# A decoder layer with 32 experts on one core: the gather leaves out empty slots, the adding up of a block moves behind the next block's first weight chunk, and ScalarE's exponential and logarithm share one table set

## The chip, the core and the metric

The kernel runs on one core of a Trainium2 chip. The core has a matrix engine (TensorE, PE in the profile, its weight loads PEld), a vector engine (VectorE, DVE), an engine for functions and copies (ScalarE, ACT), a general engine (GpSimd, POOL), an engine that issues transfers (SyncE, SP), and 16 DMA engines between HBM and the on-chip memory SBUF. PE writes its results to another on-chip memory, PSUM, of 8 banks of 512 fp32 columns for 128 partitions. Engines run their own instruction lists and meet at semaphores. The metric is the device time of one execution in microseconds (us).

## What is computed

One layer of a decoder for 288 tokens (256 of a prompt, 32 of eight samples) of width 2048, in fp32. A condition vector scales and shifts the tokens, one projection feeds two kinds of attention of 8 heads each, and w_o maps them back; a layer norm follows. Then each token goes to two of 32 experts:

```python
def hier_moe(u, w_gr, b_gr, w_er, b_er, w_gate, w_up, w_down):
    ...
    g_idx = jnp.argmax(g_logits, axis=-1)
    ...
    top_val, top_idx = lax.top_k(e_sel, TOP_K)
    gate = g_w * jax.nn.softmax(top_val, axis=-1)
    eid = g_idx[:, None] * EXPERTS_PER_GROUP + top_idx
    dense_gate = jnp.sum(jax.nn.one_hot(eid, N_EXPERTS, dtype=jnp.float32) * gate[..., None], axis=1)
    y = jnp.zeros((B * T, D), jnp.float32)
    for e in range(N_EXPERTS):
        hid = jax.nn.silu(h @ w_gate[e]) * (h @ w_up[e])
        y = y + dense_gate[:, e:e + 1] * (hid @ w_down[e])
    return y.reshape(B, T, D).astype(u.dtype)
```

The second group of heads ("stick breaking") needs log(1 + exp(-|z|)) and exp of a difference for each head.

## The kernel before

**Ahead of the experts.** All weights come through a ring of eight 1 MB slots (`ring`), loaded by SP in a fixed order. After the projections, eight heads of stick breaking run one after the other (h = 0 to 7): PE makes the logits, DVE scales them (L1541), ACT computes |z|, exp and ln(1 + ...) (L1148 to L1150), DVE adds (L1546, L1547), PE sums over keys, DVE subtracts (L1552), ACT takes the exponential (L1156), PE multiplies with the values. The sample tokens' part is woven in (L1159 to L1170 on ACT, L848 on PE). A normalisation over heads follows (ACT L1183 to L1190, DVE L1593 to L1597), then w_o and a layer norm. An activation function works only while its table set is active; the build puts an ACT_TABLE_LOAD ahead of each activation whose set is not.

**The plan.** DVE and PE route the tokens. The (token, expert) pairs are sorted by expert into blocks of B = 64 slots, an expert's pairs filling the block's slots from slot 0 up. `plan` holds each block's expert and the number of blocks (25 here), `idxs` the token of each slot (64 rows, one column for each block and one for the empty block behind the last). A slot that no pair fills has token 0.

**The loop over blocks** (L1010 on PE, L1248 on ACT, L1753 on DVE, L526 on POOL, L352 on SP). For block i:
- SP loads the expert's 12 chunks of 1 MB (`put_expert`): four of w_gate, four of w_up into `ring`, four of w_down into `mslot`. Chunk c is issued when PE has used chunk c of the block before (`moe_used`), so 12 chunks are the whole buffer.
- POOL gathers the block's 64 token rows of 8 KB from HBM into `xg` (64 partitions) by an indirect DMA (L520), as soon as PE has turned the rows of the block before out of `xg`; PE turns them one block later.
- PE multiplies the eight gate and up chunks (L1017), turns the next block's rows (`turn_rows`, L971), adds up the block before (`combine`, L999 and L1005: a matrix that holds each slot's token and weight maps 64 rows to 288 tokens), turns the hidden rows (L1028) and multiplies the four down chunks (L1036).
- DVE multiplies silu(gate) by up (`hid`, L1758), adds the five pieces of `combine` to the outputs in SBUF (`add_up`, L1744 to L1751), copies the turned hidden rows (`hT`, L1762), builds the next matrix (L1765 to L1771) and copies half of the down result (`yout`, L1773). ACT takes silu (L1252), copies the next block's turned rows (L1245) and the other half of `yout` (L1255).

The last block is added up behind the loop. A second layer norm ends the kernel: ACT copies the sample sums (L1262), POOL, DVE and ACT work on three tiles of tokens, with a logarithm and an exponential of one column for each tile (L1268, L1269).

Blocks run as hardware loops of 40 rounds, of which those from 25 on do nothing; order within an engine is the order of the code.

## Time and profile before

| what | before |
|---|---|
| median of three timed runs | 1931.15 us (1924.26 to 1936.56) |
| the profiled execution, its own time | 1920.6 us |
| its span, first to last instruction | 1918.9 us |
| mean granted TensorE clock, share of full speed | 0.938 |
| busy share of the span: PE, PEld, DVE, ACT, POOL | 86%, 50%, 28%, 13%, 6% |
| moved by the DMA engines | 545.31 MB, mean 284 GB/s |
| ACT_TABLE_LOAD in the loop | 25, 1283 ns each |

Busy shares are averages over stages with different limits. A row of a timeline gives the start and the length of a run of instructions, and in brackets how long the engine had been idle and what ended that. The chain of waits is followed back from the last instruction; its share by line says what set the end.

### The profile page before, as it was taken

The page shows a single profiled execution, that of the slowest core. Times are in us where ns is not written, and L with a number is a line of the kernel's source. Part 1 is how long each engine was busy: PE and PEld are TensorE (multiplying, and loading weights), DVE is VectorE, ACT ScalarE, POOL GpSimd, SP SyncE. Part 2 cuts the span into 40 slices and gives each one's busy share as a digit, 9 for nine tenths or more (in the row PEclk, how much of TensorE's full clock was granted, in tenths as well). Part 3 has the DMA queues.
Part 4 walks back from the last instruction along what each step waited for, and adds up shares of the span by engine and source line. Part 5 has one row for each costly group of instructions (what it writes and reads, how often), then busy time and mean ns, then how long its engine had stood idle before and what let it go on. Part 6 is the DMA issues. An engine that isn't in the chain of part 4 may idle for free.

```text
span 1918.9 us, 24776 instructions
## 1 busy us (share of the span) xinstructions
PE 1641.1 (86%) x9583; PEld 965.5 (50%) x9583; DVE 532.9 (28%) x881; ACT 250.4 (13%) x330; POOL 119.7 (6%) x155
## 2 busy tenths in 40 slices
PE   3689999999999996679968998888888888888870
PEld 0046666436787654557744564444444444444430
DVE  0010038602212213420055213131312222131328
ACT  0000012000000013630024110101010010101004
POOL 3000000001111000000020000000000000000004
PEclk8679999999989997889987999999999999999985
DMA  9988888773424353423323999999999999999961
GB/s 357 421 361 327 322 311 322 314 287 133 151 87 142 136 183 127 176 98 127 116 104 116 361 408 390 405 390 407 392 404 402 395 406 391 406 389 406 389 259 49
DMA packets 78909, 545.31 MB, mean 284 GB/s; under 512 B 9170, under 2 KB 9346, under 8 KB 16338
## 3 DMA queue, kind: packets, MB, share of 16 engines
q1 hardware_dynamic: 72146, 507.62, 67.2%
q0 software_dynamic: 6384, 34.73, 6.1%
q10 hardware_dynamic: 336, 2.36, 0.3%
q8 instruction: 31, 0.51, 0.1%
q14 instruction: 12, 0.10, 0.0%
HBM read 532.87 MB, written 11.80 MB: 284 GB/s over the span
## 4 chain that ended last, share of the span: by engine, by line
DMA 33%; PE 17%; DVE 4%; ACT 2%; issue 1%; SPq 1%; DVEq 0%; ACTq 0%
DMA ring<-w_up 33%; PE ps L893 7%; PE ps L1017 5%; PE ps L1036 1%; SPq L355 1%; PE ps L999 1%; PE ps L907 1%; ACT arena L1227 0%; DVE shift L1785 0%; DVE arena L1625 0%; PE ps L885 0%; PE ps L884 0%; DVE arena L1593 0%; PE ps L917 0%; PE ps L981 0%
## 5 line engine op out<-in xcount | busy, mean ns | idle before, releaser
L1017 PE MATMUL ps<-ring,arena 128*64 128x256 f32 x3200 | 376.4, 385 | 51.0 <-DMA ring<-w_up 45.2
L1017 PEld LDWEIGHTS ps<-ring,arena 128*64 128x64 f32 x3200 | 241.7, 138 | 190.8 <-DMA ring<-w_up 83.7
L577 PE MATMUL ps<-arena,ring 128*128 128x288 f32 x1280 | 322.0, 410 | 0.0
L577 PEld LDWEIGHTS ps<-arena,ring 128*128 128x128 f32 x1280 | 240.8, 191 | 89.8 <-issue 25.5
L1036 PE MATMUL ps<-arena 128*64 128x512 f32 x800 | 177.2, 594 | 23.6 <-DVE arena L1762 23.6
L561 PE MATMUL ps<-ring,silu_c 128*32 128x512 f32 x768 | 116.8, 719 | 53.5 <-DMA ring<-w_ada 27.4
L893 PE MATMUL ps<-arena,ring 128*128 128x288 f32 x512 | 128.3, 410 | 10.6 <-DVE arena L1593 10.6
L999 PE MATMUL ps<-arena 64*128 64x512 f32 x400 | 109.6, 633 | 24.3 <-DVE arena L1751 15.1
L1036 PEld LDWEIGHTS ps<-arena 128*64 128x64 f32 x800 | 66.2, 137 | 118.5 <-issue 90.6
L1758 DVE TENSOR_TENSOR arena<-arena,ps 128x256 f32<-128x256 f32 x25 | 10.5, 421 | 404.9 <-PE ps L1017 404.9
L893 PEld LDWEIGHTS ps<-arena,ring 128*128 128x128 f32 x512 | 98.3, 192 | 38.5 <-DVE arena L1593 11.1
L585 PE MATMUL ps<-ring,arena 128*128 128x512 f32 x256 | 113.4, 596 | 1.3 <-ACT arena L1075 1.3
L561 PEld LDWEIGHTS ps<-ring,silu_c 128*32 128x32 f32 x768 | 20.4, 118 | 130.4 <-DMA ring<-w_ada 71.0
L585 PEld LDWEIGHTS ps<-ring,arena 128*128 128x128 f32 x256 | 47.4, 190 | 62.6 <-issue 59.4
L999 PEld LDWEIGHTS ps<-arena 64*128 64x128 f32 x400 | 39.0, 190 | 75.0 <-issue 75.0
L1748 DVE TENSOR_TENSOR arena<-arena,ps 128x1024 f32<-128x1024 f32 x50 | 60.7, 1213 | 0.4 <-PE ps L999 0.4
L1773 DVE COPY arena<-ps 128x512 f32<-128x512 f32 x25 | 17.3, 691 | 148.9 <-PE ps L1036 148.9
L520 POOL DMA_INDIRECT arena<-u_rows,idx x26 | 24.3, 936 | 543.8 <-PE ps L971 542.9
L1255 ACT COPY arena<-ps 128x512 f32<-128x512 f32 x25 | 14.6, 585 | 330.1 <-PE ps L1036 330.1
L1252 ACT ACT_TABLE_LOAD x25 | 32.1, 1283 | 179.7 <-PE ps L1017 179.7
L1245 ACT COPY arena<-ps 128x1024 f32<-128x1024 f32 x26 | 26.3, 1012 | 222.1 <-PE ps L971 222.1
L1750 DVE TENSOR_TENSOR arena<-arena,ps 128x512 f32<-128x512 f32 x50 | 34.3, 687 | 54.3 <-PE ps L999 54.2
(403 smaller groups left out, 1288.8 us busy)
## 6 DMA issues: line engine op xcount, KB each, us to landing
ring<-w_gate SPq DMA_DIRECT2D x100, 1024.0 KB, 29.2
ring<-w_up SPq DMA_DIRECT2D x100, 1024.0 KB, 29.9
arena<-w_down SPq DMA_DIRECT2D x100, 1024.0 KB, 23.4
ring<-w_ada SPq DMA_DIRECT2D x96, 1024.0 KB, 8.2
ring<-w_in SPq DMA_DIRECT2D x56, 1024.0 KB, 6.3
ring<-w_o SPq DMA_DIRECT2D x16, 1024.0 KB, 5.1
ring<-cache_k SPq DMA_DIRECT2D x16, 512.0 KB, 4.2
ring<-cache_v SPq DMA_DIRECT2D x16, 512.0 KB, 4.2
```

The costliest lines, as they stand in the source:

```text
L520: nc.gpsimd.indirect_dma_start(out=xg, out_offset=None, in_=u2_rows[:], in_offset=bass.IndirectOffsetOnAxis(idx1[:, 0:1], 0)).then_inc(gat ...
L561: last = mm(ps[32 * j:32 * j + 32, 0, :], silu_c[:, t, :], ring[:, slot, 512 * j:512 * (j + 1)], start=(t == 0), stop=(t == KC - 1))
L577: last = mm(ps[:, bank, 0:T], ring[:, slot, P * t:P * (t + 1)], uT[:, t, :], start=(t == 0), stop=(t == KC - 1))
L585: mm(ps[:, 4 + i, :], uT[:, 4 * (c % 4) + t, t0:t0 + tn], ring[:, slot, 512 * t:512 * (t + 1)], start=(c % 4 == 0 and t == 0), stop=(c % 4 ...
L893: last = mm(ps[:, 4 + m % 4, 0:T], ring[:, n % SLOTS, P * k:P * (k + 1)], mixT[:, k, :], start=(k == 0), stop=(k == KC - 1))
L999: last = mm(ps[0:tn, ((7, 4), (5, 6))[j % 2][r], :], spread[rows, t0:t0 + tn], yout[rows, 512 * (j % 2):512 * (j % 2 + 1)], start=True, st ...
L1017: last = mm(ps[B * s:B * (s + 1), 2 + c // 4, 0:256], xgT[:, 4 * (c % 4) + t, :], ring[:, c, 512 * t + 256 * s:512 * t + 256 * (s + 1)], s ...
L1036: last = mm(ps[B * s:B * (s + 1), 5 + nn, :], hT[:, q % 2, B * (q // 2):B * (q // 2 + 1)], mslot[q][:, 1024 * s + 512 * nn:1024 * s + 512 ...
L1245: nc.scalar.copy(xgT, ps[:, 0:2, :].rearrange("p a (m s) -> p (a m) s", s=B)).then_inc(x_copied, 1)
L1252: A(hsil, ps[:, 2, 0:256], ACT.Silu).then_inc(sil_act, 1)
L1748: v.tensor_tensor(w, w, ps[:, 5:7, :], ALU.add).then_inc(sum_dve, 1)
L1750: v.tensor_tensor(w[:, 0], w[:, 0], ps[:, 7, :], ALU.add)
```

## The change

Three things change.

*The gather.* An index of an empty slot becomes EMPTY = 1024 instead of 0, which lies beyond the 288 rows; the indirect DMA has a bounds check of T - 1 = 287 that leaves such rows out. To make the index, DVE sums token - 1024 over the pairs of a slot and adds 1024 back (L1713 before, a tensor_scalar now); the first slot is held to at most 287 (`rowlim`), so one row is always moved. POOL fills `xg` with zeros once ahead of the first gather; a slot that is left out keeps what an earlier block left there, and its weight in the adding up is zero.

*The loop.* `combine(i)` on PE moves from behind `turn_rows` to behind chunk 0 of the gate weights; `add_up(i)` on DVE moves from behind `hid` to ahead of it.

*The tables.* ACT loads the set `natural_log_exp_and_others` once at the start, the set of Silu once ahead of the loop, and the first one again behind the loop.

```diff
@@ gather (POOL) @@
+            g.memset(rowlim[:], EMPTY)
...
+            link(g.memset(rowlim[0:1, :], T - 1.0))
...
                 nc.gpsimd.indirect_dma_start(out=xg, out_offset=None, in_=u2_rows[:],
-                                             in_offset=bass.IndirectOffsetOnAxis(idx1[:, 0:1], 0)
-                                             ).then_inc(gathered, 16)
+                                             in_offset=bass.IndirectOffsetOnAxis(idx1[:, 0:1], 0),
+                                             bounds_check=T - 1, oob_is_err=False).then_inc(gathered, 16)
...
             pool.wait_ge(tt_act, 24)
+            link(g.memset(xg, 0.0))
             gather(1)
@@ plan (DVE) @@
-                    link(v.tensor_tensor(tokid[:], tokid[:], vm, ALU.mult))
+                    link(v.tensor_scalar(tokadd[:], tokid[:], -EMPTY, None, ALU.add))
+                    link(v.tensor_tensor(tokadd[:], tokadd[:], vm, ALU.mult))
...
-            v.tensor_copy(idxs[:], ps[0:B, 4, 0:NB1]).then_inc(plan_ready, 1)
+            v.tensor_scalar(idxs[:], ps[0:B, 4, 0:NB1], EMPTY, rowlim[:, 0:1], ALU.add, ALU.min
+                            ).then_inc(plan_ready, 1)
@@ loop (PE) @@
                         last.then_inc(moe_used, 1)
+                        if c == 0:
+                            with pe.If(i > 0):
+                                combine(i)
                     turn_rows(i + 2)
-                    with pe.If(i > 0):
-                        combine(i)
@@ loop (DVE) @@
+                    with dve.If(i > 0):
+                        add_up(i)
                     dve.wait_ge(sil_act, i + 1)
...
                     v.tensor_tensor(hid, hsil, ps[:, 3, 0:256], ALU.mult).then_inc(hid_dve, 1)
-                    with dve.If(i > 0):
-                        add_up(i)
@@ tables (ACT): at the start, ahead of the loop, behind the loop @@
+            nc.scalar.preload_act_table_set("natural_log_exp_and_others")
...
+            nc.scalar.preload_act_table(ACT.Silu)
...
+            nc.scalar.preload_act_table_set("natural_log_exp_and_others")
```

How it stands in the engines' lists, where the names in brackets are the semaphores waited for. PE in the loop before, from the last up chunk (L1017, chunk 7) over the turning of rows (L971) to the first matmuls of `combine` (L999):

```order
L1017 MATMUL ps<-ring,arena 64x256 [waits moe_loaded7]
L1017 MATMUL ps<-ring,arena 64x256 x7
L968 ISA
L971 MATMUL ps<-ident,arena 128x64 [waits gathered]
L971 MATMUL ps<-ident,arena 128x64 x15
L1022 COMPARE_AND_BRANCH
L990 ISA
L993 ISA [waits spread_ready,y_evac]
L999 MATMUL ps<-arena 128x512 [waits sum_dve]
```

PE in the changed kernel, from the first gate chunk (L1023, chunk 0) to the same matmuls (now L1005):

```order
L1023 MATMUL ps<-ring,arena 64x256 [waits moe_loaded0]
L1023 MATMUL ps<-ring,arena 64x256 x7
L1028 COMPARE_AND_BRANCH
L996 ISA
L999 ISA [waits spread_ready,y_evac]
L1005 MATMUL ps<-arena 128x512 [waits sum_dve]
```

The five pieces of `combine`, with their wait for the copies of the block before (`y_evac`), now stand between chunk 0 and chunk 1; behind chunk 7 the turning of rows is followed at once by the wait for `hid_dve`.

ACT at the first two heads before: |z| (L1148), exp (L1149), ln (L1150), and the exponential of the difference (L1156):

```order
L1148 ACTIVATE arena<-arena 128x384 [waits z_dve,small_loaded]
L1149 ACTIVATE arena<-arena 128x384 [waits act_step]
L1150 ACT_TABLE_LOAD
L1150 ACTIVATE arena<-arena 128x384 [waits act_step]
L1148 ACTIVATE arena<-arena 128x384 [waits z_dve]
L1149 ACT_TABLE_LOAD
L1149 ACTIVATE arena<-arena 128x384 [waits act_step]
L1150 ACT_TABLE_LOAD
L1150 ACTIVATE arena<-arena 128x384 [waits act_step]
L1156 ACT_TABLE_LOAD
L1156 ACTIVATE arena<-arena 128x384 [waits d_dve]
```

The same place in the changed kernel (L1156 to L1158, and L1164):

```order
L1156 ACTIVATE arena<-arena 128x384 [waits z_dve,small_loaded]
L1157 ACTIVATE arena<-arena 128x384 [waits act_step]
L1158 ACTIVATE arena<-arena 128x384 [waits act_step]
L1156 ACTIVATE arena<-arena 128x384 [waits z_dve]
L1157 ACTIVATE arena<-arena 128x384 [waits act_step]
L1158 ACTIVATE arena<-arena 128x384 [waits act_step]
L1164 ACTIVATE arena<-arena 128x384 [waits d_dve]
```

The four table loads are gone. In the whole list of ACT there were 35 of them, one in the loop among these; three are left: at the start, ahead of the loop, behind it.

## Rows read from the trace of the kernel before

**Rows 1.** The page, 40 slices of the span: what the DMA engines moved, GB/s.
```profile
GB/s 357 421 361 327 322 311 322 314 287 133 151 87 142 136 183 127 176 98 127 116 104 116 361 408 390 405 390 407 392 404 402 395 406 391 406 389 406 389 259 49
```

**Rows 2.** Chain of waits: start us, us, what held the chain (line, pieces).
```profile
1078.37 13.81 PE ps L1017 x128
...
1107.80 13.81 PE ps L1017 x128
...
1216.82 30.86 DMA ring<-w_up
...
1282.60 30.77 DMA ring<-w_up
```

**Rows 3.** Timeline of a block: start, us, engine, line, tiles [idle before <- releaser].
```profile
1240.27 1.95 PE L1017 MATMUL ps<-ring,arena 128*64 128x256 f32 x16 [0.52 <-DMA ring<-w_up]
...
1247.73 1.95 PE L1017 MATMUL ps<-ring,arena 128*64 128x256 f32 x16 [0.54 <-DMA ring<-w_up]
...
1250.54 0.69 PE L999 MATMUL ps<-arena 64*128 64x512 f32 x1
...
1255.82 1.06 PE L1005 MATMUL ps<-arena 64*32 64x512 f32 x8 [0.34 <-DVE arena L1751]
...
1258.20 7.09 PE L1036 MATMUL ps<-arena 128*64 128x512 f32 x32 [0.95 <-DVE arena L1762]
...
1265.32 0.69 DVE L1773 COPY arena<-ps 128x512 f32<-128x512 f32 x1 [5.96 <-PE ps L1036]
```

**Rows 4.** Short windows: us, busy of PE, PEld, DVE, ACT, POOL; clock, DMA share, GB/s.
```profile
1242.50:1245.00 2.50, 1.95 (x16) 1.06 (x16) 0.00 (x0) 0.00 (x0) 0.00 (x0) 1.00 1.02 423
...
1255.00:1257.50 2.50, 1.91 (x14) 0.38 (x10) 2.36 (x4) 0.00 (x0) 0.00 (x0) 1.00 1.08 331
1257.50:1260.00 2.50, 1.80 (x10) 0.81 (x12) 1.83 (x6) 0.00 (x0) 0.00 (x0) 1.00 1.00 246
```

**Rows 5.** All instructions of line 520, the gather; then issue to landing.
```profile
L520 POOL DMA_INDIRECT arena<-u_rows,idx x26: 922/922/1187, 1036.0 to 1810.2; - x26
...
DMA to landing us min/median/max: 5.1/9.2/9.9
```

**Rows 6.** ACT among the heads: one group (busy us, mean ns, idle before), then its timeline.
```profile
L1150 ACT ACT_TABLE_LOAD x8 | 10.3, 1283 | 0.1
...
748.53 1.28 ACT L1150 ACT_TABLE_LOAD   x1
749.82 0.52 ACT L1150 ACTIVATE arena<-arena 128x384 f32<-128x384 f32 x1
...
773.79 0.52 ACT L1156 ACTIVATE arena<-arena 128x384 f32<-128x384 f32 x1 [0.38 <-DVE arena L1552]
```

**Rows 7.** Timeline of the same stretch, DVE, then one row of PE.
```profile
781.57 0.62 DVE L1541 TENSOR_SCALAR arena<-ps,biasb 128x384 f32<-128x384 f32 x1 [0.32 <-PE ps L798]
...
800.97 3.11 DVE L1544 TENSOR_TENSOR arena<-arena,negmask 128x384 f32<-128x384 f32 x1
...
825.77 4.96 DVE L1593 SCALAR_TENSOR_TENSOR arena<-arena,normw 128x2304 f32<-128x2304 f32 x1 [9.64 <-ACT arena L1190]
...
789.71 7.19 PE L848 MATMUL ps<-ring,arena 128*32 128x128 f32 x255 [1.39 <-ACT arena L1170]
```

**Rows 8.** Waits in the loop, 21 blocks: engine, line, waited for: us, times, longest.
```profile
DVE arena L1758 <- PE ps L1017: 344.5, 21, 16.7
```

**Rows 9.** Timeline of the end.
```profile
1895.25 1.28 ACT L1269 ACT_TABLE_LOAD   x1
...
1896.76 4.49 POOL L549 TENSOR_TENSOR arena<-arena,ring 128x2048 f32<-128x2048 f32 x1
1896.78 4.48 DVE L1785 SCALAR_TENSOR_TENSOR shift<-bnag,rs 128x1 f32<-128x1 f32 x1 [1.88 <-ACT rs L1269]
...
1905.02 1.28 ACT L1269 ACT_TABLE_LOAD   x1
```

**Rows 10.** Timeline of POOL at the start: a memset of 384 columns.
```profile
8.16 0.44 POOL L418 MEMSET causal<- 128x384 f32 x1
```

More of the change, by code:

```diff
@@ L47 @@
 NEG_BIG = -1.0e30
+EMPTY = 1024.0
 def layer(nc, xT, cT, w_ada, b_adaT, b_g2, w_in, w_o, w_r, b_r, lb_logits, norms, sb_bias,
@@ L268, in layer @@
         tokid = sb("tokid", [P, 3])
+        tokadd = sb("tokadd", [P, 3])
+        rowlim = sb("rowlim", [B, 1])
         iotab = sb("iotab", [P, B])
@@ L1703, in _ @@
                 if k == 0:
-                    link(v.tensor_tensor(tokid[:], tokid[:], vm, ALU.mult))
+                    link(v.tensor_scalar(tokadd[:], tokid[:], -EMPTY, None, ALU.add))
+                    link(v.tensor_tensor(tokadd[:], tokadd[:], vm, ALU.mult))
                 for i in range(3):
                     v.tensor_scalar(rsel[k][:, i, :], iotab[:], sl[:, i:i + 1], None, ALU.is_equal)
-                    last = v.tensor_scalar(bsel[k][:, i, :], iotab[:, 0:NB1], blk[:, i:i + 1], tokid[:, i:i + 1],
+                    last = v.tensor_scalar(bsel[k][:, i, :], iotab[:, 0:NB1], blk[:, i:i + 1], tokadd[:, i:i + 1],
                                            ALU.is_equal, ALU.mult)
```

## The prediction

> **What bounds the kernel now.** I read the slices of the page first: of 40 slices of 48 us, numbers 23 to 38 move about 400 GB/s, numbers 10 to 22 between 87 and 183 [rows 1]. So there are two regimes: an expert loop of some 770 us that streams, and a stretch ahead of it that does not. The chain of waits names the loop's limit: its first blocks belong to PE, one every 1107.80 - 1078.37 = 29.43 us, and from the fourth on it is a DMA of an up-projection chunk, two blocks in 1282.60 - 1216.82 = 65.78 us, 32.89 each [rows 2]. PE needs 29.43 and gets its weights every 32.89: the loop is bound by its stream.
>
> Next, what the stream consists of. While PE waits chunk by chunk, one lands every (1247.73 - 1240.27) / 3 = 2.487 us [rows 3]; twelve take 29.84. The other 3.05 us are neither weights nor an idle queue: narrow windows show 423 GB/s as a rule, but 331 and 246 in two of 2.5 us, with the DMA engines fully busy and the clock at its upper level [rows 4]. That is where the gather, issued by POOL and 9.2 us in flight [rows 5], moves its 64 rows of 8 KB. Its own 0.52 MB at 423 GB/s take 1.24 us, and the missing (92 + 177) x 2.5 us = 0.67 MB are 1.59 us more: 2.83 of the 3.05. **A gather costs the stream about 3 us a block.**
>
> Ahead of the loop I looked for table loads that somebody waits for. Eight stand in the stretch of heads directly ahead of a logarithm, 1.28 us each with 0.02 us of air around them [rows 6].
>
> **The change, part by part.**
>
> *Gather.* Each of the 288 tokens takes two experts: 576 rows in 25 blocks of 64 slots. The reference's routing of its inputs fills the blocks of gathers 3 to 26 (those that lie in the stream; the last one is empty but for its forced first slot) with 545 rows of 1,536, 35%. No row of before shows a skipped slot, so I bound it. If all of the 3.05 us scales with rows, 1.08 stay. If rows are dealt to the 16 engines four neighbours each, the fullest engine still carries four in most blocks: a chunk is 8 packets of 8 KB an engine, 0.31 us each, so 1.24 stay, and of the remaining 1.81 the 35%, 0.64: 1.88. Between these I take 1.5, so 1.55 are saved, 24 times: **-37 us** (from -28 to -47). The lower end for rows that are skipped but cost as before is nothing; that is a rival below.
>
> By the Trainium skill, SBUF — State Buffer, section on the DMA port swizzle, partitions 0 to 63 reach only 8 of 16 DMA ports, and partitions 0-3 and 32-35 share one. No row shows ports; the 246 GB/s with busy engines would agree. By that rule the fullest port counts: 8 rows before, and with slots filled from the bottom 4.6 on average (13 of the 24 blocks leave it 4, six above 35 rows leave it 8): 3.05 x 4.6 / 8 = 1.76 stay and -31 us come out instead of -37.
>
> Does PE become the bound? The new block is about 31.3 us of stream against 29.43 of PE; the stream stays ahead by 1.9.
>
> *Rows added up behind chunk 0.* The combine runs from 1250.54 to 1256.88, 6.3 us, between the last up chunk and the down projection [rows 3]. Moved, it is the same PE work. Its new wait is for the two copies of the block before; they end 0.7 us after the last down matmul [rows 3], and chunk 0 covers 13.81 / 8 = 1.73 us [rows 2]. Without that cover it costs 0.7 a block. Behind it on PE stand chunks 1 to 7, and so SP's refills of their ring slots; with 12 slots and a stream that is behind, they wait in the queue anyway. On DVE the five additions move ahead of the product of gate and up, which is needed some 12 us later. So nothing changes per block while the stream rules. What changes is the end: after the last up chunk the combine no longer stands before the down projection. PE enters chunk 1 up to 6.3 us late and makes up 2.49 - 1.73 = 0.76 at each of seven chunks, 5.3; it may reach the last one 1 to 3 us behind. **-4 us** (from -3 to -6).
>
> *Tables, stretch of heads.* The loads ahead of the exponential of the differences (eight fewer, line 1156) are covered: ACT still waits 0.38 us for DVE after one [rows 6]. Of those on line 1150, head 3's is covered because DVE then waits for PE, all but 0.32 [rows 7]; head 5's runs beside 7.19 us of sample matmuls [rows 7]; head 6's beside a DVE addition of 3.11 us [rows 7]. So of eight, five count, with two on line 1149 and one on line 1163: 8 x 1.28 = 10.3, and 0.3. Of the four in the normalisation the second pair runs beside the DVE operation of 4.96 us that the first pair leads to [rows 7]. Of the first pair the one ahead of the exponential counts whole, the one ahead of Ln in part, since the sums behind it come from PE: between 1.28 and 2.57, I take 1.8. Sum **-12.4 us**; all 13 that could count would give -16.7, the eight alone without the rest -10.
>
> The Trainium skill, ScalarE: Activation LUTs, section on what a table load costs, gives 1283 ns and a drain of about 1380 ns for each switch. The rows agree with the first and leave no place for the second: 0.02 us stand between the loads and their neighbours [rows 6]. With the drain these parts would bring 19 us more.
>
> *Tables, loop.* 25 loads of 1.28 us go, worth nothing: DVE's product waits for PE's last chunk, up to 16.7 us, not for ACT [rows 8]. Without that cover they would be 32 us. The loads of the decay and of the first layer norm stand in PE-bound or DVE-bound stretches and count nothing as well.
>
> *Tables, end.* Five loads could count: one ahead of the sample sums and the four around the variances, like 1905.02, which the last four DVE operations wait for [rows 9]. But after the load at 1895.25 a DVE operation on one column takes 4.48 us and ends with POOL's 4.49 us beside it, so that this load may only move a wait [rows 9]. Two to five loads: -2.6 to -6.4, I take four, **-5.1 us**.
>
> *Added.* A POOL memset of 2048 columns ahead of the first gather: 384 columns take 0.44 us and the fixed part is small [rows 10], so I estimate 1.9 us; the first gather then moves 9 rows instead of 64 and lands sooner. From 0 to +1.9, I take **+0.8**. One dependent DVE operation of 0.2 us lies in DVE's slack ahead of PE's selection matmuls, worth nothing, or 0.2 without it. The two preloads ahead of and behind the loop stand where ACT waits.
>
> **Sum.** -37 - 4 - 12.4 - 5.1 + 0.8 = -58 us. The profiled execution took 1920.6 (span 1918.9): 1863. The median of the three timed runs is 1931.15, 10.5 above it; with the same saving, **1873 us**.
>
> **Rivals.**
> - *The port rule decides* (SBUF — State Buffer, as above): the fullest lane, not the number of rows, sets the price. For it: 64 rows disturb far more than their bytes. Against it: no row tells lanes apart. -31 instead of -37: 1879 us.
> - *Skipping saves nothing.* The price is not one of rows but of a software gather as such (descriptors still made and walked). For it: of 3.05 us only 1.24 are bytes. Against it: in the slow windows the engines are busy, which looks like packets. Then -58 + 37 = -21: 1910 us.
> - *The tables bring a drain more*: 1854 us. The rows speak against it.
> - *Slower: the ring starves.* Combine now stands ahead of chunks 1 to 7, so their slots come free some 6 us later. If the additions there wait longer than before, PE's block grows until PE is the bound. To be 1% slower, 19 us, and lose the 17 of the tables, a block needs 32.89 + 36 / 24 = 34.4 us, 5 us more than the 29.43 it takes with the same work. Against it: the only new wait is covered by 1 us. It would give 1950 us.
>
> **Chances and range.** The forecast, a gather that still costs 1.1 to 1.7 us, 0.61, with its own range of 1858 to 1884 by that and by the tables' bounds; the port rule 0.20; no saving from skipping 0.12; the drain 0.02; slower 0.05. A measurement of this kernel tells about 1% from no change, 19 us. Faster by more than that is all but the last and a good half of the third: 0.88; within 1%: 0.07; slower: 0.05. The range holds the forecast and the port rule with the ends of the bounds: -47 - 16.7 - 6.4 - 6 = -76 below, -28 - 3 - 10 - 2.6 + 1.9 = -42 above, from 1931, and 6 us for the spread of the timed runs (1924.26 to 1936.56): 1848 to 1895. It leaves out the other two, 0.17.
>
> **What would show it.** The gathers' period in the middle of the loop: 31.3 us if the price is 1.5, 31.6 by the port rule, 32.9 if skipping brings nothing, above 33 with PE without waits for DMA if the ring starves. Short windows where the gather lands should stay near 400 GB/s in blocks of few rows. After the last up chunk PE should go on to the down projection within 3 us. From the first head's table load at 748.53 to the start of that long DVE operation at 825.77 it should take 12 us less. I am wrong if the period does not fall below 32, or if it falls below 30.5, where PE is the bound.

## The result, and the profile after

| what | before | after |
|---|---|---|
| median of the timed runs | 1927.7 us (1922.38 to 1936.56, 4 runs) | 1872.5 us (1871.95 to 1877.9, 3 runs) |
| ratio, 95% interval | | 0.9728 (0.9702 to 0.9753) |
| the profiled execution, its own time | 1920.6 us | 1872.5 us |
| its span | 1918.9 us | 1870.7 us |
| mean granted TensorE clock | 0.938 | 0.935 |

A fourth run of the changed kernel took 6913 us and is left out, since nothing like it came again; counted in, it makes the median 1875.2, which some expectations below start from. The forecast was 1873 us with a range of 1848 to 1895. By the medians 55.2 us were gained, by the ratio 52, where 58 had been summed; between the two profiled executions it is 48.1.

The spans can be laid beside each other by stages. The marks are rows of the timelines: ACT's first operation on the heads' |z|, the first long DVE operation behind the heads, the first gate matmul of the loop and the end of its last down matmul. The last column is worked out from the two before it.

| stage, us | before | after | difference |
|---|---|---|---|
| start to the heads | 747.4 | 751.9 | +4.5 |
| heads | 78.3 | 68.4 | -10.0 |
| from there to the expert loop | 226.5 | 225.0 | -1.4 |
| expert loop | 804.6 | 769.3 | -35.3 |
| to the end | 62.1 | 56.1 | -6.0 |

The first row is not put down to the change: of it only table loads (two fewer) and a small memset act there, and over the profiles of the twelve kernels below this stage ended between 745.6 and 755.2 us with no relation to what was edited.

The page of the changed kernel: what moved in 40 slices of the span, in GB/s, the packets by size, and the queue of the gather with its packets, MB and share.

```profile
GB/s 354 421 384 314 314 322 328 311 296 157 149 91 135 97 198 184 99 163 133 113 158 96 214 415 410 411 414 421 412 400 416 398 414 411 402 422 414 415 214 50
DMA packets 78909, 536.41 MB, mean 287 GB/s; under 512 B 10257, under 2 KB 10433, under 8 KB 17425
...
q0 software_dynamic: 6384, 25.83, 4.3%
```

The loop's slices, which read 389 to 408 before [rows 1], read 398 to 422. With all 64 slots moved in every block that queue moves 34.73 MB (so in the first of the price experiments below), now 25.83. Its packets are 6384 in both: a row that is left out still makes one, of under 512 B instead of 8 KB (10257 of that size instead of 9170; the 1087 more are the rows left out).

All instructions of line 525, the gather, with the time from issue to landing:

```profile
L525 POOL DMA_INDIRECT arena<-u_rows,idx x26: 982/1166/1167, 1031.0 to 1772.1; - x26
...
DMA to landing us min/median/max: 3.5/7.7/9.4
```

The median landing fell from 9.2 [rows 5] to 7.7 us, while POOL's own part of a gather grew from 922 to 1166 ns; nobody waits for that. It is the new order of the loop that does it and not the bounds check: with the move alone, without the check, it is 1188 ns, with the gather alone, in the old order, 964.

The chain of waits in the loop (start us, us, what held the chain):

```profile
1078.85 12.24 PE ps L1023 x112
...
1108.32 12.24 PE ps L1023 x112
...
1314.52 12.24 PE ps L1023 x112
...
1341.97 27.86 DMA ring<-w_gate
...
1405.94 27.80 DMA ring<-w_gate
```

Before, PE's own work held the chain for three blocks, then the loads of up chunks did [rows 2]. Now PE holds it for nine blocks, one every 1108.32 - 1078.85 = 29.47 us, up to 1314.52. Then the stream takes over, two blocks in 1405.94 - 1341.97 = 63.97 us. What is waited for there is the **first gate** chunk, no longer an up chunk. Over 15 blocks, from the one that ends in that first wait up to the start of the last, the period is 31.56 us on average (473.4 us in all), between 30.15 where one row was gathered and 32.4 to 32.9 where more than 35 were. Twelve chunks take 29.84 [rows 3], so that 1.7 us of a gather's 3.05 stay in these blocks.

PE in a block that it bounds (start, us, engine, line; idle before and its releaser in brackets):

```profile
1218.02 1.93 PE L1023 MATMUL ps<-ring,arena 128*64 128x256 f32 x16
1219.88 1.99 PE L1005 MATMUL ps<-arena 64*128 64x512 f32 x8
1222.49 2.26 PE L1005 MATMUL ps<-arena 64*128 64x512 f32 x8 [0.62 <-DVE arena L1764]
1225.08 1.06 PE L1011 MATMUL ps<-arena 64*32 64x512 f32 x8 [0.34 <-DVE arena L1764]
1226.08 6.26 PE L1023 MATMUL ps<-ring,arena 128*64 128x256 f32 x56
```

The combine stands behind chunk 0 and starts without a wait; the 0.62 and 0.34 us inside it were there before, the latter in [rows 3].

And PE at the end of the last block:

```profile
1802.42 5.37 PE L1043 MATMUL ps<-arena 128*64 128x512 f32 x24 [0.70 <-DVE arena L1775]
1811.07 3.55 PE L1043 MATMUL ps<-arena 128*64 128x512 f32 x8 [3.28 <-DMA arena<-w_down]
```

The down projection begins within 3 us of the last up chunk, as forecast, but the last chunk's eight matmuls wait 3.28 us for their transfer. Before, all 32 ran in one piece at this place:

```profile
1849.72 7.09 PE L1036 MATMUL ps<-arena 128*64 128x512 f32 x32 [0.95 <-DVE arena L1762]
```

So the wait is new, and the experiments on the late load go after it.

Short windows with the columns of [rows 4], around a gather of one row (issued at 1240.5, its packet at 1244.9) and one of 57 rows (issued at 1487.5, packets from 1491.8 to 1495.9):

```profile
1243.00:1245.50 2.50, 2.50 (x14) 1.02 (x12) 0.00 (x0) 0.00 (x0) 0.00 (x0) 1.00 1.02 420
1245.50:1248.00 2.50, 2.50 (x18) 1.13 (x15) 0.28 (x1) 0.28 (x1) 0.18 (x1) 1.00 1.02 420
...
1491.50:1494.00 2.50, 2.48 (x14) 0.78 (x12) 0.00 (x0) 0.00 (x0) 0.00 (x0) 1.00 1.05 292
1494.00:1496.00 2.00, 0.94 (x6) 0.06 (x2) 0.69 (x1) 0.59 (x1) 0.00 (x0) 1.00 1.00 242
```

One row leaves no mark; 57 rows dig the same hole as 64 did [rows 4].

### The profile page after: what moved, and what is told of

The parts are those of the page before. It is cut to its first block, busy times and chain, and to the rows that moved or that the text cites. A ratio compares the mean times of both kernels' runs of the same rounds, so it can differ in the third digit from the quotient of the medians.

```text
span 1870.7 us, 24750 instructions
## 1 busy us (share of the span) xinstructions
PE 1638.1 (88%) x9583; PEld 957.2 (51%) x9583; DVE 533.5 (29%) x882; ACT 178.4 (10%) x274; POOL 128.8 (7%) x158
## 2 busy tenths in 40 slices
DMA packets 78909, 536.41 MB, mean 287 GB/s; under 512 B 10257, under 2 KB 10433, under 8 KB 17425
## 3 DMA queue, kind: packets, MB, share of 16 engines
q0 software_dynamic: 6384, 25.83, 4.3%
## 4 chain that ended last, share of the span: by engine, by line
PE 33%; DMA 12%; DVE 5%; issue 2%; SPq 2%; ACT 1%; DVEq 0%; ACTq 0%
PE ps L1023 13%; DMA ring<-w_gate 11%; PE ps L899 7%; PE ps L1043 6%; PE ps L1005 2%; SPq L358 2%; DMA arena<-w_down 2%; DVE arena L1764 1%; PE ps L977 1%; PE ps L1011 1%; ACT arena L1235 1%; PE ps L913 0%; DVE arena L1635 0%; PE ps L891 0%; PE ps L890 0%
## 5 line engine op out<-in xcount | busy, mean ns | idle before, releaser
L1023 PE MATMUL ps<-ring,arena 128*64 128x256 f32 x3200 | 360.9, 384 | 24.9 <-DMA ring<-w_gate 22.8
L1023 PEld LDWEIGHTS ps<-ring,arena 128*64 128x64 f32 x3200 | 230.6, 138 | 171.0 <-DMA ring<-w_gate 35.7
L1005 PE MATMUL ps<-arena 64*128 64x512 f32 x400 | 110.3, 649 | 23.0 <-DVE arena L1764 14.7
L1005 PEld LDWEIGHTS ps<-arena 64*128 64x128 f32 x400 | 35.4, 194 | 89.1 <-issue 89.1
L525 POOL DMA_INDIRECT arena<-u_rows,idx x26 | 30.0, 1154 | 544.3 <-PE ps L977 543.4
L470 POOL TENSOR_TENSOR arena<-arena,seqmask 32x1024 f32<-32x1024 f32 x8 | 15.3, 1907 | 415.4 <-DVE arena L1384 415.2
L1261 ACT ACTIVATE arena<-ps 128x256 f32<-128x256 f32 x25 | 9.6, 384 | 353.5 <-PE ps L1023 353.5
```

The source lines that it names most:

```text
L525: nc.gpsimd.indirect_dma_start(out=xg, out_offset=None, in_=u2_rows[:], in_offset=bass.IndirectOffsetOnAxis(idx1[:, 0:1], 0), bounds_check ...
L1005: last = mm(ps[0:tn, ((7, 4), (5, 6))[j % 2][r], :], spread[rows, t0:t0 + tn], yout[rows, 512 * (j % 2):512 * (j % 2 + 1)], start=True, st ...
L1023: last = mm(ps[B * s:B * (s + 1), 2 + c // 4, 0:256], xgT[:, 4 * (c % 4) + t, :], ring[:, c, 512 * t + 256 * s:512 * t + 256 * (s + 1)], s ...
```

## Experiments: the change in its parts

**The gather alone.** The change without its other two parts:

```diff
-            nc.scalar.preload_act_table_set("natural_log_exp_and_others")
...
-            nc.scalar.preload_act_table(ACT.Silu)
...
-            nc.scalar.preload_act_table_set("natural_log_exp_and_others")
...
-                        if c == 0:
-                            with pe.If(i > 0):
-                                combine(i)
                     turn_rows(i + 2)
+                    with pe.If(i > 0):
+                        combine(i)
```

(and `add_up(i)` on DVE back behind `hid`.)

> The gather's part alone, on the kernel before; combine and table loads stand where they stood. Measure: the loop, from the first gate matmul to the end of the last down matmul, 804.6 us before and 769.3 after the whole change. Theory G (the gather is all of the loop's gain, moving the combine brings nothing, because the last w_down chunk is then waited for instead): 768 to 771 us, 34 to 36 less than before. Theory M (as forecast, the move gives 4 us of its own): 773 us. Total by G some 35 us under before, by M 31.

Measured: 1892.2 us against 1924.87, ratio 0.9825 (0.9776 to 0.9873). The loop took 768.8 us against 804.6: 35.8 us, all of the loop's gain in the full change. Dealt over 24 gathers that is 1.49 each, so 1.56 of 3.05 would stay on average; in the first blocks PE is the bound, and what a gather costs the stream there is not seen.

**The move alone.** The kernel before with these lines only:

```diff
+                        if c == 0:
+                            with pe.If(i > 0):
+                                combine(i)
                     turn_rows(i + 2)
-                    with pe.If(i > 0):
-                        combine(i)
```

(with `add_up(i)` ahead of `hid` on DVE.)

> The moved combine alone; gather of 64 rows and table loads as before. Theory G: loop 803 to 806 us, as before, period 32.9 in the middle, DMA waits moved from chunks 3 to 7 to chunk 0, and the last w_down chunk waited for. Theory M: about 800 us. The rival of the forecast that the ring starves: period above 33.5, loop over 815.

Measured: 1928.09 us, ratio 1.0021 (0.9995 to 1.0046, ten runs): nothing. The loop is 802.7 us instead of 804.6, and its last down matmuls run in one piece:

```profile
1852.71 7.09 PE L1037 MATMUL ps<-arena 128*64 128x512 f32 x32 [0.70 <-DVE arena L1763]
```

**The tables alone.** The kernel before with the three preload lines of the change.

> The shared table set alone. Forecast: 12.4 us less among the heads (first head's |z| to the long DVE operation, 78.3 before), 5.1 at the end (last down matmul to the span's end, 62.1 before), nothing in the loop. After the whole change these were 68.4 and 56.1, 10.0 and 6.0 less; theory: the 2.4 us that the heads lack belong to TensorE's lower clock between them, so this kernel shows 66 to 69 and 56. A drain of 1.38 us a load would show as 20 us or more less among the heads.

Measured: 1907.01 us, ratio 0.9903 (0.9875 to 0.9931), some 18 us. The heads took 65.5 us instead of 78.3 (66 to 69 had been expected), the end 56.1 instead of 62.1. In the chain of waits of its end (start, us, what held it), the DVE operation on one column that took 4.48 us beside POOL's long one [rows 9] is now short:

```profile
1883.54 1.19 DVE shift L1788
```

It ends, as before, together with a long POOL operation, but now with the one ahead of that, of which only a last part is left:

```profile
1880.20 4.51 POOL L548 TENSOR_TENSOR arena<-arena,ring 128x2048 f32<-128x2048 f32 x1 [2.29 <-ACT arena L1274]
```

So the load ahead of it did not only move a wait: it pushed the operation beside the whole of the next long POOL operation. Some 1.2 us of this come back at the next tile, where the operation on one column takes 1.33 us beside POOL's, and took 0.15 before. In the full change the two are 1.19 and 1.33 us as well.

## Experiments: what ate the move

The last stage needs a 2 MB pair of rows (`ln2b`), which POOL fetches into the first two ring slots as soon as the last up chunk is used. Before, it fell among the last down chunks too (it took 11.6 us to land, and alone it takes 7.3, below), but PE came to them only behind the combine, by when they were there. With the combine ahead of chunks 1 to 7 PE comes to them sooner.

**The late load, later.** The changed kernel with

```diff
-            pool.wait_ge(moe_used, nblocks * MOE_CHUNKS + SLOTS)
+            pool.wait_ge(moe_used, nblocks * MOE_CHUNKS + MOE_CHUNKS)
```

> The changed kernel with one edit: the 2 MB load of the last layer norm's rows waits for the last down chunk instead of the last up chunk. Theory G: in the changed kernel that load shares the DMA engines with the last four w_down chunks, which are waited for now; without it the last down matmuls end 3 to 4 us sooner after the last gate chunk (34.8 us from its first matmul to the last down end in the changed kernel, 31 here). Rival: the last chunks are late from the gathers, then nothing changes. If the load is needed before it lands, the end grows by up to 5 us instead.

Measured: 1866.75 us, ratio to before 0.9693 (0.9641 to 0.9746), 6 us below the changed kernel's median of another call. The load's row in the list of transfers (KB, median us to landing), of the changed kernel and then of this one:

```profile
ring<-ln POOLq DMA_DIRECT2D x1, 2048.0 KB, 11.3
```

```profile
ring<-ln POOLq DMA_DIRECT2D x1, 2048.0 KB, 7.3
```

It lands in 7.3 us when it is alone. And the end of the loop in the chain of waits of this kernel:

```profile
1754.11 25.44 DMA ring<-w_gate
1779.59 1.95 PE ps L1023 x16
...
1802.19 7.10 PE ps L1043 x32
```

All 32 down matmuls run in one piece. From the first chunk of the last block to the end of its down matmuls it takes 1809.3 - 1779.6 = 29.7 us, against 34.8 in the changed kernel; 2 MB at the 423 GB/s of [rows 4] are 5.0 us.

**The late load with the old order.** This separates the move from the load:

```diff
-                        if c == 0:
-                            with pe.If(i > 0):
-                                combine(i)
                     turn_rows(i + 2)
+                    with pe.If(i > 0):
+                        combine(i)
```

on top of the kernel above (`add_up(i)` back as well).

> The changed kernel with the loop's old order (rows added up after the last up chunk) and the 2 MB load of the last stage waiting for the last down chunk; rows lie in the slots as in the changed kernel. If the move is worth its 4 us once that load is out of the way, the loop is about 768 to 769 us here against the 764.4 of the kernel with the new order and the late load, and the time about 1871 against 1866.75. If the late load alone was the gain, the loop is 764 and the time 1867. From the first chunk of the last block to its last down matmul, 30 us either way.

Measured: 1869.24 us (1864.55 to 1875.26), ratio 0.9703 (0.9649 to 0.9757). The times are too near each other to decide, but the profiles do: its loop took 768.6 us, with the new order 764.4. So the move is worth 4.2 us once the load is out of its way, and with the load where it was the load takes 4.9 back (769.3). In the old order the early load costs next to nothing: the loop of the gather alone, with the load where it was, took 768.8, which is 0.2 more than here. In the chain of waits of this kernel the stream takes over after five blocks,

```profile
1193.66 13.83 PE ps L1023 x128
1207.50 28.15 DMA ring<-w_up
```

in the one with the new order, counted in the same way, after eight:

```profile
1299.00 5.38 PE ps L1043 x24
...
1310.13 27.84 DMA ring<-w_gate
```

The old order takes eight chunks in 13.81 us, while the stream brings one in 2.487 [rows 2, 3], eight in 19.9: at the start of a block PE must have some 6 us of chunks in stock. The new order takes them in 8.06 + 12.24 = 20.3 us (1218.02 to 1226.08 above, then the 112 matmuls of the chain), at the stream's own pace, and lives on a smaller stock.

## Experiments: what a gather's rows cost

In four kernels every gather moves a fixed set of slots, whatever the routing; all other indices lie beyond the bound. The additions of combine were shortened to an eighth of their columns there, so that PE does not become the bound. One run each, with a profile. The edit, for the third of them:

```diff
+            keep(rowm[:], [[-4, 8]], 0, 1, 0.0, ALU.is_equal)
...
+            link(v.tensor_reduce(rowlim[:, 0:1], rowm[:], AX, ALU.add))
```

`rowlim` decides for each slot whether its index stays below the bound; the patterns are all 64 slots, slots 0-3 with 32-35, every fourth slot from 0 to 28, and slots 0 to 31.

> The changed kernel with every gather moving the same slots, whatever is filled, and with the adding up cut to 64 of each 512 columns, which takes some 4 us of PE off a block, so that the stream is the bound from the start; what is left out is that part of the sums. Here all 64 slots: both theories expect the period of before, 32.9 us, 3.0 over twelve chunks (29.84).

> As the kernel with all 64 slots, but only slots 0 to 3 and 32 to 35 are moved, 8 rows. Price over 29.84 us a block. Theory P (price in proportion to rows): 0.4 us. Theory E (rows dealt to engines in fours, the fullest engine decides): four rows on each of two engines, 1.2 us. Theory L (what decides is a lane into SBUF that these eight slots share): eight rows, 2.4 to 3.0 us, as all 64. By the Trainium skill, SBUF - State Buffer, section on the DMA port swizzle, these eight share one port.

> As before, but slots 0, 4, 8 to 28, 8 rows, each in a group of four of its own. Theory P: 0.4 us. Theories E and L: one row on the fullest, 0.3 us. Against the 8 rows in two groups this tells whether place or number sets the price.

> As before, but slots 0 to 31, 32 rows. Theory P: 1.5 us. Theories E and L: four rows on the fullest, 1.2 us; L expects this to be far below the 8 rows of slots 0 to 3 and 32 to 35, P far above.

PE's timeline in the four, in this order: chunks that end a wait, by which the period is read.

```profile
1337.90 1.95 PE L1024 MATMUL ps<-ring,arena 128*64 128x256 f32 x16 [0.53 <-DMA ring<-w_up]
...
1469.88 1.95 PE L1024 MATMUL ps<-ring,arena 128*64 128x256 f32 x16 [0.53 <-DMA ring<-w_up]
```

```profile
1393.65 1.95 PE L1024 MATMUL ps<-ring,arena 128*64 128x256 f32 x16 [0.53 <-DMA ring<-w_up]
...
1490.72 1.95 PE L1024 MATMUL ps<-ring,arena 128*64 128x256 f32 x16 [0.73 <-DMA ring<-w_up]
```

```profile
1307.76 1.95 PE L1024 MATMUL ps<-ring,arena 128*64 128x256 f32 x16 [0.55 <-DMA ring<-w_gate]
...
1490.69 1.95 PE L1024 MATMUL ps<-ring,arena 128*64 128x256 f32 x16 [0.56 <-DMA ring<-w_gate]
```

```profile
1306.52 1.95 PE L1024 MATMUL ps<-ring,arena 128*64 128x256 f32 x16 [0.53 <-DMA ring<-w_gate]
...
1494.93 1.95 PE L1024 MATMUL ps<-ring,arena 128*64 128x256 f32 x16 [0.53 <-DMA ring<-w_gate]
```

Four blocks lie between the first pair, three between the second, six between the others. What is above the 29.84 us of twelve chunks is the gather's price. The last column is the median of the gather's rows in the lists of transfers.

| slots moved | rows | period, us | price, us | issue to landing, us | time of the one run, us |
|---|---|---|---|---|---|
| all 64 | 64 | 33.0 | 3.2 | 9.7 | 1904.68 |
| 0-3 and 32-35 | 8 | 32.36 | 2.5 | 8.5 | 1884.98 |
| 0, 4, ... 28 | 8 | 30.49 | 0.65 | 7.0 | 1853.45 |
| 0 to 31 | 32 | 31.40 | 1.56 | 8.0 | 1867.14 |

The second and the third move the same eight rows' worth of bytes, and one costs four times the other; 32 rows cost less than the eight of the second. So the place of the rows decides more than their number. The number is not nothing: the first and the second load the fullest lane alike, with 64 rows and with 8, and lie 0.7 apart. And no theory had all four: the third costs some twice what each gave, and the fourth what the price by number gave. If the eight rows of 8 KB in the second all go through one of the 16 engines, at the 0.31 us a packet of the prediction, they take 2.5 us: its price as it was measured. By the Trainium skill, SBUF — State Buffer, section on the DMA port swizzle, partitions 0-3 and 32-35 share one port; the pair of runs agrees with that.

The changed kernel's own blocks show the same steps. Its chunks 0 that wait for the stream, from two stretches of the loop:

```profile
1402.58 1.95 PE L1023 MATMUL ps<-ring,arena 128*64 128x256 f32 x16 [3.02 <-DMA ring<-w_gate]
1433.79 1.95 PE L1023 MATMUL ps<-ring,arena 128*64 128x256 f32 x16 [1.52 <-DMA ring<-w_gate]
1465.02 1.95 PE L1023 MATMUL ps<-ring,arena 128*64 128x256 f32 x16 [1.56 <-DMA ring<-w_gate]
1497.94 1.95 PE L1023 MATMUL ps<-ring,arena 128*64 128x256 f32 x16 [3.00 <-DMA ring<-w_gate]
...
1687.45 1.95 PE L1023 MATMUL ps<-ring,arena 128*64 128x256 f32 x16 [1.10 <-DMA ring<-w_gate]
1718.52 1.95 PE L1023 MATMUL ps<-ring,arena 128*64 128x256 f32 x16 [1.18 <-DMA ring<-w_gate]
1749.69 1.95 PE L1023 MATMUL ps<-ring,arena 128*64 128x256 f32 x16 [1.48 <-DMA ring<-w_gate]
1779.84 1.95 PE L1023 MATMUL ps<-ring,arena 128*64 128x256 f32 x16 [0.47 <-DMA ring<-w_gate]
```

Blocks with 21 and 30 rows (read from the bytes of the gather's queue) pay 1.37 and 1.39 us above 29.84, the block with 57 rows 3.08; then 6 and 16 rows pay 1.23 and 1.33, and one row 0.31. From 6 to 30 rows the price hardly moves, and it doubles where slots 32 to 35 are filled too. These are one, four and eight rows on the fullest lane, if four neighbours share one with the four slots 32 further on, at 0.31 to 0.39 us a row.

Short windows of the second and the first kernel, while their rows are in flight:

```profile
1402.00:1405.50 3.50, 1.17 (x6) 0.17 (x2) 0.00 (x0) 0.00 (x0) 0.00 (x0) 1.00 1.01 400
```

```profile
1411.90:1416.20 4.30, 1.23 (x6) 0.17 (x2) 0.00 (x0) 0.00 (x0) 0.00 (x0) 1.00 1.04 248
```

Eight rows in one lane leave 400 GB/s, and yet cost 2.5 us. That the other engines go on while a chunk is complete only with its slowest part would explain it; no row shows single engines. So the hole in the GB/s, by which the prediction explained the price, shows only one of two ways in which rows cost.

**Rows dealt over the lanes.** If the fullest lane alone sets the price, dealing a block's rows over the groups of four slots should lower it:

```diff
+                link(v.tensor_scalar(tmp3, sl, float(B // 4), None, ALU.is_ge))
+                for j in range(2, 4):
+                    link(v.scalar_tensor_tensor(tmp3, sl, float(j * B // 4), tmp3, ALU.is_ge, ALU.add))
+                link(v.tensor_scalar(sl, sl, 4.0, None, ALU.mult))
+                link(v.scalar_tensor_tensor(sl, tmp3, 1.0 - B, sl, ALU.mult, ALU.add))
```

> The changed kernel, with the rows of a block dealt over the 64 slots in strides (slot s becomes 4 x (s mod 16) + s / 16), so that consecutive rows fall into different groups of four slots; five more small DVE operations for each of the two choices in the routing. What is computed stays the same. Lane theory (slots 4j to 4j+3 and 32+4j to 32+4j+3 share one lane, and the fullest lane sets the price, some 0.31 to 0.4 us a row): over gathers 3 to 26 the fullest lanes carry 83 rows instead of 114, 31 x 0.35 = 11 us less of stream; PE's 29.43 a block is near, so that 7 to 11 come through: loop 769 to about 760 us, time about 1867 (after: 1875), late periods of about 31 instead of 31.6. Proportional theory (the number of rows sets the price): nothing changes, loop 769, or 1 us more in the routing.

Measured: 1873.74 us, ratio 0.9725 (0.9692 to 0.9758): as the changed kernel. The loop took 772.1 us, 2.8 more, and the last 15 periods are 31.73 on average instead of 31.56. For dealt rows the theory of the fullest lane fails; the price by number, which expected no change, comes nearer here, but it does not fit the steps above. What the trace shows is that the gather's landing did not come sooner but later: 8.1 us against 7.7.

```profile
arena<-u_rows,idx POOLq DMA_INDIRECT x26, 8.1
```

And the windows around a gather of 21 rows, dealt and, in the changed kernel, in slots 0 to 20:

```profile
1429.10:1431.80 2.70, 2.70 (x14) 1.04 (x12) 0.00 (x0) 0.00 (x0) 0.00 (x0) 1.00 1.04 294
```

```profile
1429.30:1431.10 1.80, 1.80 (x10) 0.67 (x8) 0.00 (x0) 0.00 (x0) 0.00 (x0) 1.00 1.12 314
```

Each window spans the rows' first to last packet: 2.7 us instead of 1.8, at no better rate. Across the kernels the price goes with the landing: 0.65 at 7.0 us, 1.56 at 8.0, 1.9 at 8.1 (the dealt rows, 31.73 - 29.84), 2.5 at 8.5, 3.2 at 9.7; only the changed kernel, 1.7 at 7.7, falls out of this order. That a row is more often followed by weight packets when its neighbours lie elsewhere, so that its lane is held longer, would explain it, but is only argued. Which order of slots would be cheapest for 20 rows stays open.

**Dealt rows, late load, and the old order with them.** The two kernels are the one above with the wait on `MOE_CHUNKS`, the second also with the old order of the loop (both diffs are shown above).

> As the run before, and the 2 MB load for the last stage waits for the last down chunk of the last block instead of its last up chunk. If that load takes the down chunks' share of the DMA engines, the stretch from the first chunk of the last block to the end of its down matmuls is about 30 us instead of 35 and the time falls 4 to 8 us more, to about 1860; if the load is a matter of indifference, it stays at 1867.

> As the run before, with the loop's old order (a block's rows added up after the next block's last up chunk). If the move is worth the 4 us forecast once the late load no longer hides it, this run is 3 to 6 us slower than the one with the new order, all of it behind the first chunk of the last block (34 to 35 us instead of 30); if the move is worth nothing whatever the load does, both are within 2 us.

Measured: 1865.51 us (1864.03 to 1871.34), ratio 0.969 (0.9654 to 0.9727), and 1871.11 us (1867.9 to 1873.52), ratio 0.9712 (0.9676 to 0.9748). The late load brings 8 us again by the medians, 4.5 of them in the loop, and the loops of the two orders stand 767.6 to 772.1 us: the move is worth 4.4 here as well. But the place that was expected was wrong: from the first chunk of the last block on, both take about 30 us (29.7 and 30.3). The old order loses its time earlier, where PE waits for up chunks. The kernel with the late load and undealt rows (1866.75) and the dealt one (1865.51) cannot be told apart; either is 6 to 7 us below the change, by its ratio or its median.

## Why the prediction was right, step by step

**The bound.** The loop was bound by its stream, and a gather cost it 3 us: the kernel that moves all 64 slots in every block has 33.0 us a block, the kernel before 32.89 [rows 2].

**Gather, -37: right in size, in part by luck.** Measured -35.8 (gather alone) and -35.3 in all of the loop. The price of 1.5 us that was chosen came out as 1.56 when the gain is dealt over 24 gathers. But it was the middle of two bounds, and hardly a block pays it: the steps are 0.31, some 1.33 and some 2.84 us (the mean of 57 rows, 3.08, and of 36 rows, 2.59 between the waits at 1529.12 and 1561.55). That is the port rule's count of rows on the fullest lane, so the rival held at 0.20 is nearer to the mechanism than the forecast. Its -31 fell short because it priced four rows at half of 3.05, 1.53. An estimate with its own count of the 24 blocks and the prices of the steps (13 times 1.33, six times 2.84, three single rows, and some 1.7 and 1.0 for blocks of 33 and of 3 rows) leaves 38 of 73 us: 35 are saved, as measured. For dealt rows the same count fails, so what a lane does to the stream stays open. The rival by which skipping saves nothing is out: periods of 32.4 us and more are seen only where a gather has more than 35 rows.

**PE as the bound.** "The stream stays ahead by 1.9", as the longer of the two, held for 15 blocks. It overlooked that a slower drain lets the stock of chunks that the loop starts with last longer: PE bounded nine blocks, not three. With the old order and the same gather it bounds five (two kernels), so the rest is the new order's. The rival of the starving ring did not come: where PE waits it waits for the stream, and never above 33 us a block.

**Move of the combine, -4: right size, lost on the way.** With the late load out of the way it gives 4.2 and 4.4 us (two pairs of profiles). In the change it gave nothing. Alone it gave 1.9 us of loop and nothing in the time (1.0021), and there the load did not eat it: the last down matmuls did not wait. What can be seen there is that PE waited 2.98 us for the first chunk of the last block, the granted clock then read 0.62 over 4.5 us, and that block took 31.3 us, against 29.7 with the late load moved. Whether this is all that is missing is not shown. The step that failed is "what changes is the end": PE did reach the down projection early, but the last down chunk was then still in flight, and the 2 MB load that POOL issues at the last up chunk, which the combine had covered, was not looked at. It costs 4.9 us.

**Tables, heads, -12.4.** From the table load ahead of the first head's logarithm to the long DVE operation it took 77.2 us (748.53 to 825.77, [rows 6, 7]). After, from that logarithm itself, on ACT and on DVE,

```profile
753.03 0.52 ACT L1158 ACTIVATE arena<-arena 128x384 f32<-128x384 f32 x1
```

```profile
820.29 4.84 DVE L1603 SCALAR_TENSOR_TENSOR arena<-arena,normw 128x2304 f32<-128x2304 f32 x1 [9.62 <-ACT arena L1198]
```

it is 67.3, so 10.0 less instead of 12. The stage varies by itself: without the new tables it took 78.3 us (before), 83.2 (gather alone) and 83.2 (move alone), with them between 65.4 and 69.9. So 12.4 lies inside what the runs show (the means are 81.6 without and 67.7 with them, 13.9 apart), and one pair of profiles does not settle a term of this size. A possible cause of the spread is seen in a window of the changed kernel in this stage, where the granted clock (the first of the last three columns) was 0.50, the lower of its two levels, with PE busy throughout:

```profile
795.00:800.00 5.00, 5.00 (x27) 4.08 (x20) 2.81 (x2) 1.57 (x3) 4.02 (x1) 0.50 1.02 429
```

The row is of a stretch in which matmuls stand on the way; in the kernel before, the window of the same figures read 1.00, though its work stood some 5 us further back there. It is not shown to make up the 2.4 us: the tables alone, with the shorter heads of 65.5 us, read 0.57 in the same window.

**Tables, loop, 0: right.** ACT lost 25 loads of 1.28 us there, and the loop of the tables alone is 805.7 us against 804.6.

**Tables, end, -5.1.** Measured -6.0, in the change and with the tables alone. The doubt whether the load at 1895.25 only moved a wait [rows 9] is settled: it cost its time and 3.3 us more, since the DVE operation behind it ran into POOL's, less the 1.2 that come back at the next tile.

The drain that the Trainium skill, ScalarE: Activation LUTs, section on what a table load costs, adds to each switch would, by an estimate from its figure, have made 19 us more of these terms. The tables alone gained 18 in all, where the loads' own 1.28 us made 17.5: no run here shows the drain.

**Memset and index, +0.8.** From the heads to the loop it took 225.0 us against 226.5: no cost can be seen.

**The sum.** -58 was forecast, -48.2 stands between the two spans. Ahead of the heads 4.5 us were lost, where the change does next to nothing, in the loop 5.7 (mostly the move), in the heads 2.4; the end and the part ahead of the loop gave 3 more than forecast. The medians gained 55.2, over runs before that spread by some 14. That 1873 was met to half a microsecond is luck: the misses of the parts and a median before that came out at 1927.7 instead of 1931.15 cancel.

## What to carry to other kernels

When a step is moved so that the engine stops waiting there, list the transfers that are issued by counts along the old order: here a 2 MB load keyed to "last up chunk used" had always fallen among the last chunks of the stream, unnoticed behind the combine; with the combine gone it took back all that the move gave, and one constant gave it back. Leaving out rows of a gather saves by where the rows lie more than by their number: price a gather in the stream's period with a few fixed patterns before rearranging slots. And a term of a few microseconds in a stage whose clock changes from run to run needs several profiles, not a pair.

## What the runs showed of the hardware

- Eight rows of 8 KB into partitions 0-3 and 32-35 cost the weight stream 2.5 us, into every fourth of partitions 0 to 28 0.65 us; 32 rows into partitions 0 to 31 cost 1.56 us. Filled from partition 0 up, 1 row cost 0.31, 6 to 30 rows 1.23 to 1.39, 57 rows 3.08.
- In the first of these the engines together still moved 400 GB/s. A low rate in a short window is thus not needed for a stream to be late.
- Dealing rows over the lanes lengthened their time in flight (2.7 us instead of 1.8 for 21 rows), against what the fullest lane's count says.
- Rows left out by a bounds check moved next to no bytes (25.83 MB in the queue instead of 34.73) but kept their packets (6384 in both).
- An indirect DMA of 64 rows took POOL 922 ns in the old order of the loop and 1188 in the new one; the bounds check made it 964 and 1166.
